# Block scores of the prompt computed per query in small matmuls, and the sample gates spread by a matmul, in a stage of a hybrid decoder step

## The chip, the cores and the metric

The kernel runs on one core of one Trainium2 chip. The metric is the device time of one execution in microseconds (us), the median of several runs. A core has a matrix engine (TensorE, PE in the profile; its weight loads are listed apart as PEld), a vector engine (VectorE, DVE), a scalar engine (ScalarE, ACT), GpSimd (POOL) and SyncE (SP), which here only issues DMA transfers. Each engine runs its own list of instructions in order and waits for the others on semaphores. SBUF is the on-chip memory with 128 partitions, PSUM the memory that TensorE writes.

## The reference, cut to what matters

One decoder layer for a prompt of 1024 tokens and for 8 samples of 4 new tokens with a history of 8192. Half of the heads do dilated window attention (mixer A), the other half native sparse attention (mixer B) with three branches that are weighted by gates. The change touches two things of mixer B.

For the prompt, the compressed branch: every query of 8 heads scores 16 compressed keys (one for each block of 64 tokens), adds a bias, masks blocks that have not ended, takes a softmax and multiplies the compressed values.

For the samples, the gates of all three branches:

```
gates = jax.nn.sigmoid(gates.astype(jnp.float32)).reshape(n, t, G_B, R_B, 3)

def _nsa_compressed(q, kc, vc, q_pos, bias_b):
    nbc = kc.shape[1]
    blk_end = (jnp.arange(nbc) + 1) * NSA_BLOCK - 1
    rel = q_pos[:, None] - blk_end[None, :]
    bias = jnp.transpose(bias_b[_t5_bucket(rel)], (0, 2, 3, 1))
    logits = jnp.einsum('ntgrd,nkgd->ntgrk', q, kc, ...) * ATT_SCALE + bias
    probs, _ = _masked_softmax(logits, (rel >= 0)[None, :, None, None, :])
    out = jnp.einsum('ntgrk,nkgd->ntgrd', probs, vc.astype(jnp.float32))
    return out, jnp.sum(probs, axis=3)
```

Here n is 1, t is 1024 for the prompt, g is 2 and r is 4 (8 query heads on 2 key heads), d is 64 and k is 16.

## The kernel before, in words

The program is a row of stages with a barrier of all engines between two of them: `front` (projections and compression), `compressed_and_dilated` (the stage of this change), `sample_selected`, `prompt_attention` and `ffn`. All numbers are 32-bit floats; TensorE does each such matmul in two passes, and the profile lists each pass as one MATMUL with one LDWEIGHTS. A transpose with the identity is one pass.

`compressed_and_dilated` interleaves three works in steps s = 0 to 11, an order that is written out by hand in a loop of each engine.

- The dilated attention of the 8 samples is the backbone. In step s, `keys(s, h)` transposes the keys of sample s in 8 banks of four 128 x 128 blocks (h = 0 and 1 are the halves) into two PSUM banks in turn (`psT`). ScalarE copies banks 0, 2, 4, 6 and VectorE banks 1, 3, 5, 7 to SBUF (`KT`, in the tile `turned`; `key_copies`). TensorE writes a bank again only when its last copy is done. `scores(n, h)` then multiplies. After the fourth sample VectorE takes a maximum over `psS`, ScalarE the exponential (`PR`), and `probs(g)` and `values(g)` follow.
- The compressed branch of the samples gives the choice of blocks (`choice`, its result is `pen`). SyncE waits for `pen` before it loads the rest of the values (items 12 to 15 of `load`), and from item 13 on also for `values(0)`. At the end SyncE issues the loads for the next stage (window keys, biases), and the stage ends when the last of its issues is done.
- The compressed branch of the prompt uses what is left. `qp` holds the queries with channels on partitions: chunk ch of four has two heads of 64 channels, 1024 tokens wide. `kbd` holds the 16 compressed keys twice, block diagonal, so that one matmul scores two heads and makes 32 rows. In step 3 `prompt_scores` makes the scores with `kbd` as weights (128 x 32) and the queries moving (512 columns); four chunks stand side by side in the array (`tile_position`). ScalarE and VectorE copy the two halves to `SQ`, which takes the place of chunk 0 of `qp`. In step 4 `prompt_scores_by_query` transposes the eight 128 x 128 blocks, so that queries are on partitions, and VectorE adds the bias of distance (`prompt_sums`), which makes `Lp`, 8 tiles of 128 queries with 8 heads and 16 blocks. `prompt_maxima` takes the maxima and subtracts them, ScalarE takes the exponential at the start of step 5, `prompt_weights` normalizes.

The sample gates: 768 numbers of one row in DRAM are sent by one DMA to all 128 partitions of `graw`. ScalarE takes the sigmoid in step 2, and `gates_and_block_logits` of VectorE sorts them with 24 small copies into `GB`. `graw` is a view of the tile `early`.

Of the kernel before, what the change touches and what calls it, by code (L numbers as in the profile page):

```python
# [9 lines left out]
ACT = mybir.ActivationFunctionType  # L10
AXX = mybir.AxisListType.X

P = 128
D = 1024
KC = D // P
SEQ = 1024
# [1190 lines left out]
def compressed_and_dilated(nc, io, scr, mixB, GB, Qb, pre, ident, kcs, vcs, knew, s_nl, s_mixed, stores):  # L1207
# [13 lines left out]
    with ExitStack() as stack:  # L1221
        m = Mem(nc, stack, "cd")
        flip = m.sb("flip", [P, P])
        rsum = m.sb("rsum", [P, 2, NR])
        qs = m.sb("qs", [P, 4, RS])
# [5 lines left out]
        graw = early[:, :].rearrange("p (a n) -> p a n", a=2)  # L1231
# [25 lines left out]
        SQ = qp[:, 0, :]  # L1257
# [31 lines left out]
        s_ps = m.sem("prompt_scores_by_block")  # L1289
        s_pa = m.sem("prompt_scores_copied_by_act")  # L1290
        s_pd = m.sem("prompt_scores_copied_by_dve")
# [69 lines left out]
        def _(pool):  # L1361
# [9 lines left out]
            pool.wait_ge(s_z, 4)  # L1371
# [13 lines left out]
        def _(sp):  # L1385
            def load(i):
                if i >= NS:
# [5 lines left out]
                         bass.AP(scr["gates"].tensor, SEQ * 24, [[0, P], [1, RS * 24]])).then_inc(s_c, 16)  # L1393
# [44 lines left out]
        def _(pe):  # L1438
# [78 lines left out]
            def gates_and_block_scores():  # L1517
                pe.wait_ge(s_c, LOADS)
                pe.wait_ge(s_z, 4)
# [13 lines left out]
            def prompt_scores():  # L1533
# [5 lines left out]
                for half in range(2):  # L1539
                    for ch in range(4):  # L1540
                        mm = pe.matmul(psX[32 * ch:32 * ch + 32, half, :], kbd[:, ch // 2, :],
                                       qp[:, ch, half * 512:half * 512 + 512], start=True, stop=True,
                                       tile_position=(0, 32 * ch))
                    mm.then_inc(s_ps, 1)

            def prompt_scores_by_query():
                pe.wait_ge(s_pa, 1)
                pe.wait_ge(s_pd, 1)
                for qt in range(QT):
                    pe.transpose(psX[:, qt // 4, (qt % 4) * P:(qt % 4) * P + P], SQ[:, qt * P:qt * P + P],  # L1550
                                 ident[:, :]).then_inc(s_po, 1)
# [50 lines left out]
            for s in range(NB + 4):  # L1602
# [9 lines left out]
                if s == 4:  # L1612
                    prompt_scores_by_query()
# [33 lines left out]
        def _(act):  # L1647
# [3 lines left out]
            for s in range(NB + 4):  # L1651
                if s < NB:
                    key_copies(act, copy, d_ca, 0, s, 0)
                if s == 5:
                    act.wait_ge(s_d, 3)
                    nc.scalar.activation(Lp[:, :, :, :], Lp[:, :, :, :], ACT.Exp).then_inc(s_e, 1)
# [24 lines left out]
                if s == 3:  # L1681
# [5 lines left out]
                    act.wait_ge(s_ps, 2)  # L1687
                    copy(SQ[:, 0:512], psX[:, 0, :]).then_inc(s_pa, 1)
# [13 lines left out]
        def _(dve):  # L1702
            def gates_and_block_logits():
                dve.wait_ge(s_a, 1)
# [87 lines left out]
            for s in range(NB + 4):  # L1792
# [25 lines left out]
                if s == 4:  # L1818
                    prompt_sums()
# [32 lines left out]
                if s == 4:  # L1852
                    prompt_maxima()
                    block_probs()
# [1539 lines left out]
```

## Time and profile before

| | |
|---|---|
| median of 3 runs | 2150.55 us (2150.45 to 2152.93) |
| the profiled execution's own time | 2152.93 us |
| its span, first to last instruction | 2151.2 us |
| PE busy | 2051.5 us (95%) |
| PEld busy | 1339.3 us (62%) |
| DVE busy | 1082.9 us (50%) |
| ACT busy | 521.6 us (24%) |
| POOL busy | 532.7 us (25%) |
| mean granted TensorE clock | 0.981 of full speed |

Times inside the execution are counted from the span's start. The stage of the change lies between 512.5 and 635.5 us. A row of the timeline gives the start, the length, the engine, the line, the operation, output <- input with their shapes, the number of instructions merged in it, and in brackets for how long the engine had been idle and who released it. "issue" names no releaser: the engine waited for nothing that the profile shows.

### The profile page before, as it was taken

What the parts mean: (1) busy time and instruction counts of PE and PEld (TensorE: products, weight loads), DVE (VectorE), ACT (ScalarE), POOL (GpSimd) and SP (SyncE); (2) the same over time, 40 slices, a digit from 0 to 9 for tenths busy, and PEclk for the clock granted to TensorE, in tenths of its full rate; (3) what the DMA queues carried; (4) which work ended last, traced back from release to release, by engine and by line L of the source; (5) the groups of instructions that cost most, each with busy time, mean ns of one, the idle gap of its engine ahead of it and who ended that gap; (6) DMA issues with size and microseconds to landing.
All of it is one profiled execution on the core that took longest, in us unless ns stands there. A gap on an engine that the chain in (4) does not pass through costs nothing. (4 is left out here: it accounts for less than half of the span.)

```text
span 2151.2 us, 31682 instructions
## 1 busy us (share of the span) xinstructions
PE 2051.5 (95%) x12366; PEld 1339.3 (62%) x12366; DVE 1082.9 (50%) x2484; ACT 521.6 (24%) x1106; POOL 532.7 (25%) x714
## 2 busy tenths in 40 slices
PE   6999999998977997999999999999999999999998
PEld 3445466665545665666676447888888888734443
DVE  5035455411525455666776226767777765611452
ACT  4111011001323344766766111011111111000011
POOL 1444234202024551012222101222322222303110
PEclk9999999998999998999999999999999999999999
DMA  8477678643697996222251414666556622601100
GB/s 219 138 241 258 243 294 305 236 170 109 231 339 290 402 396 226 99 67 68 82 155 39 133 60 156 215 208 204 196 196 211 220 79 60 227 12 30 42 40 39
DMA packets 156393, 373.05 MB, mean 173 GB/s; under 512 B 36981, under 2 KB 95085, under 8 KB 138189
## 3 DMA queue, kind: packets, MB, share of 16 engines
q1 hardware_dynamic: 126580, 149.89, 22.2%
q0 software_dynamic: 25280, 149.44, 18.0%
q10 hardware_dynamic: 4384, 71.68, 9.5%
q8 instruction: 99, 1.62, 0.3%
q14 instruction: 50, 0.41, 0.1%
HBM read 343.68 MB, written 98.60 MB: 206 GB/s over the span
## 5 line engine op out<-in xcount | busy, mean ns | idle before, releaser
L2773 PE MATMUL ff_ps<-ff_hx,whole_aw 128*128 128x264 f32 x2464 | 550.5, 386 | 0.9 <-DVE ff_hx L3074 0.9
L2773 PEld LDWEIGHTS ff_ps<-ff_hx,whole_aw 128*128 128x128 f32 x2464 | 467.1, 190 | 80.8 <-issue 1.4
L802 DVE STREAM_TRANSPOSE whole_space<-whole_space 128x512 f32<-128x512 f32 x256 | 155.3, 674 | 153.7 <-PE in_psH L611 142.0
L575 PE MATMUL in_ps<-in_w,in_xT 128*128 128x512 f32 (+1 forms) x512 | 201.5, 547 | 0.0
L1155 DVE CUSTOM_DVE_ANT_0 pa_L<-pa_psS,whole_space 128x512 f32<-128x512 f32 (+3 forms) x288 | 138.9, 532 | 46.8 <-PE pa_psS L1008 45.8
L575 PEld LDWEIGHTS in_ps<-in_w,in_xT 128*128 128x128 f32 x512 | 95.0, 190 | 94.2 <-issue 87.6
L1135 ACT ACTIVATE pa_L<-pa_L,pa_nm 128x640 f32<-128x640 f32 (+3 forms) x192 | 141.9, 741 | 32.3 <-DVE pa_nm L1165 30.5
L2799 PE MATMUL ff_ps<-ff_hx,whole_space 128*128 128x512 f32 x336 | 148.0, 593 | 0.0
L700 ACT ACTIVATE in_yout<-in_ps 128x128 f32<-128x128 f32 (+5 forms) x88 | 41.0, 479 | 378.8 <-PE in_ps L575 199.6
L3155 DVE SCALAR_TENSOR_TENSOR whole_space<-whole_space,ff_kept 128x1024 f32<-128x1024 f32 x88 | 123.3, 1401 | 3.1
L611 PE MATMUL in_psH<-whole_space 128*64 128x256 f32 (+1 forms) x1152 | 121.6, 364 | 0.0
L1008 PE MATMUL pa_psS<-whole_space,pa_qT 64*128 64x512 f32 (+3 forms) x576 | 115.3, 506 | 5.6 <-POOL pa_qT L1079 5.6
L589 PE MATMUL in_ps<-in_xT,in_w 128*128 128x352 f32 x384 | 117.6, 463 | 0.0
L2799 PEld LDWEIGHTS ff_ps<-ff_hx,whole_space 128*128 128x128 f32 x336 | 63.6, 190 | 80.6 <-issue 80.6
L2996 ACT ACTIVATE whole_space<-whole_space 128x1056 f32<-128x1056 f32 x22 | 23.8, 1084 | 368.6 <-DVE whole_space L3157 368.6
L1029 PE MATMUL pa_psT<-whole_ident,pa_L 128*128 128x128 f32 x816 | 111.9, 281 | 0.2 <-DVE pa_PT L1181 0.2
L1029 PEld LDWEIGHTS pa_psT<-whole_ident,pa_L 128*128 128x128 f32 x816 | 87.3, 141 | 39.5 <-issue 18.3
L2728 PE MATMUL ff_ps<-whole_space 128*128 128x512 f32 x256 | 111.2, 593 | 0.0
L1049 PE MATMUL pa_psO<-pa_PT,whole_space 128*64 128x128 f32 x1632 | 110.3, 279 | 0.9 <-DVE pa_tmp L1193 0.5
L1129 ACT ACTIVATE pa_PT<-pa_psT 128x512 f32<-128x512 f32 (+2 forms) x182 | 91.9, 541 | 75.9 <-PE pa_psT L1029 74.3
L611 PEld LDWEIGHTS in_psH<-whole_space 128*64 128x64 f32 x1152 | 74.9, 137 | 47.1 <-issue 13.0
L589 PEld LDWEIGHTS in_ps<-in_xT,in_w 128*128 128x128 f32 x384 | 71.8, 190 | 42.2 <-issue 3.8
(411 smaller groups left out, 2579.9 us busy)
## 6 DMA issues: line engine op xcount, KB each, us to landing
out_new_a_k_s<-in_cache_a_k ACTq DMA_DIRECT2D x8, 4088.0 KB
out_new_a_v_s<-in_cache_a_v ACTq DMA_DIRECT2D x8, 4088.0 KB
whole_aw<-in_w_up SPq DMA_DIRECT2D x44, 512.0 KB
in_w<-in_w_in SPq DMA_DIRECT2D x5, 2048.0 KB
whole_space<-in_cache_a_k SPq DMA_DIRECT2D x8, 1024.0 KB
whole_space<-in_cache_a_v SPq DMA_DIRECT2D x8, 1024.0 KB
ff_hx<-in_w_down SPq DMA_DIRECT2D x14, 512.0 KB, 4.7
whole_space<-in_x_prompt SPq DMA_DIRECT2D x13, 512.0 KB, 4.0
```

What stands on the lines that cost most here:

```text
L575: mm = pe.matmul(ps[0:n, b, 0:width], xT[:, k, t * P:t * P + n], w[:, at % WBUF, k, 0:width], start=(k == 0), stop=(k == KC - 1))
L589: mm = pe.matmul(ps[:, b, 0:n], w[:, at % WBUF, k, c * P:c * P + P], xT[:, k, r0:r0 + n], start=(k == 0), stop=(k == KC - 1))
L611: mm = pe.matmul(psH[dh * HD:dh * HD + HD, r % 2, o0:o0 + n], w1[:, kv, t16, dh, :], rows[:, dh, t, :], start=(t16 == 0), stop=(t16 == 15) ...
L802: last = dve.transpose(put[:, dh, :, k * HD:k * HD + HD].rearrange("p t (g b) -> p t g b", g=2), got[:, :, :, dh, :])
L1008: pe.matmul(psS[:, c % 2, h, 0:w], qT[r, i, qt * P:qt * P + P], kT[i][r, j0 * P + k0:j0 * P + k0 + w], start=True, stop=True).then_inc(s_q ...
L1029: mm = pe.transpose(psT[:, b % 3, (x - x0) * P:(x - x0) * P + P], turned, ident[:, :])
L1135: nc.scalar.activation(x, x, ACT.Exp, bias=nm[:, s, h:h + 1], scale=1.0, accum_out=sm[:, s, h:h + 1]).then_inc(s_ex, 1)
L1155: dve.tensor_tensor_reduce(L[:, u % 3, h, 512 * x:512 * x + n], psS[:, c % 2, h, 0:n], T[it % 2][:, h, SEQ - w + 512 * x:SEQ - w + 512 * x ...
L2728: mm = pe.matmul(ps[:, j % 6, :], mixT[:, k, t * P:t * P + P], wo[:, k, half * 512:half * 512 + 512], start=(k == 0), stop=(k == KC - 1))
L2773: mm = pe.matmul(ps[:, bank_of(x, j, g), 0:H2], aw[:, j % 2, at, k, :], hx[:, bt, k, g * H2:g * H2 + H2], start=(k == 0), stop=(k == KH - 1))
L2799: mm = pe.matmul(ps[:, b, :], a[:, k, :], wd(k0 + k)[:, c0:c0 + 512], start=(k == 0), stop=(k == KD - 1))
L3155: dve.scalar_tensor_tensor(out=out[:, 0:SEQ], in0=U[:, v, k:k + SEQ], scalar=tap(k), in1=out[:, 0:SEQ], op0=ALU.mult, op1=ALU.add)
```

## The change

Five edits, all in `compressed_and_dilated`:

1. `prompt_scores` takes the queries as weights (128 x 128) and `kbd` as the moving side (32 columns), for each of 8 query tiles and 4 chunks. The result has queries on partitions at once. `prompt_scores_by_query`, the tile `SQ` and the two copies into it go.
2. `prompt_sums` and `prompt_maxima` of VectorE, which stood at two places of step 4, stand behind the bias copy at the end of step 3, in `prompt_logits`.
3. The exponential of `Lp` on ScalarE stands at the end of step 4 and not at the start of step 5.
4. The gates come by DMA to one partition only; ScalarE takes the sigmoid there; TensorE spreads them over 128 partitions with two matmuls of a row of ones (1 x 128 weights, 384 columns); VectorE's 24 copies read them from PSUM.
5. GpSimd fills the row of ones, one memset more.

```
+        ones = m.sb("ones", [1, P])
-        graw = early[:, :].rearrange("p (a n) -> p a n", a=2)
+        graw = early[0:1, :].rearrange("p (a n) -> p a n", a=2)
...
+            pool.memset(ones[:, :], 1.0).then_inc(s_z, 1)
-            pool.wait_ge(s_z, 4)
+            pool.wait_ge(s_z, 5)
...
-                         bass.AP(scr["gates"].tensor, SEQ * 24, [[0, P], [1, RS * 24]])).then_inc(s_c, 16)
+                         bass.AP(scr["gates"].tensor, SEQ * 24, [[0, 1], [1, RS * 24]])).then_inc(s_c, 16)
...
             def gates_and_block_scores():
                 pe.wait_ge(s_c, LOADS)
-                pe.wait_ge(s_z, 4)
+                pe.wait_ge(s_z, 5)
+                pe.wait_ge(s_a, 1)
+                for a in range(2):
+                    pe.matmul(psX[:, a, 0:RS * 24 // 2], ones[:, :], graw[:, a, :], start=True, stop=True)
                 pe.transpose(psX[:, 0, 384:512], rows[:, :], ident[:, :]).then_inc(s_pe, 1)
...
                 pe.wait_ge(s_v, 7)
-                for half in range(2):
+                for qt in range(QT):
                     for ch in range(4):
-                        mm = pe.matmul(psX[32 * ch:32 * ch + 32, half, :], kbd[:, ch // 2, :],
-                                       qp[:, ch, half * 512:half * 512 + 512], start=True, stop=True,
-                                       tile_position=(0, 32 * ch))
-                    mm.then_inc(s_ps, 1)
-
-            def prompt_scores_by_query():
-                pe.wait_ge(s_pa, 1)
-                pe.wait_ge(s_pd, 1)
-                for qt in range(QT):
-                    pe.transpose(psX[:, qt // 4, (qt % 4) * P:(qt % 4) * P + P], SQ[:, qt * P:qt * P + P],
-                                 ident[:, :]).then_inc(s_po, 1)
+                        o = (qt % 4) * P + ch * 32
+                        mm = pe.matmul(psX[:, qt // 4, o:o + 32], qp[:, ch, qt * P:qt * P + P], kbd[:, ch // 2, :],
+                                       start=True, stop=True)
+                    mm.then_inc(s_po, 1)
...
-                if s == 5:
-                    act.wait_ge(s_d, 3)
-                    nc.scalar.activation(Lp[:, :, :, :], Lp[:, :, :, :], ACT.Exp).then_inc(s_e, 1)
...
-                    act.wait_ge(s_ps, 2)
-                    copy(SQ[:, 0:512], psX[:, 0, :]).then_inc(s_pa, 1)
+                if s == 4:
+                    act.wait_ge(s_d, 3)
+                    nc.scalar.activation(Lp[:, :, :, :], Lp[:, :, :, :], ACT.Exp).then_inc(s_e, 1)
...
             def gates_and_block_logits():
-                dve.wait_ge(s_a, 1)
+                dve.wait_ge(s_pe, 1)
                 for a in range(2):
-                    got = graw[:, a, :].rearrange("p (b t g n) -> p b g t n", b=4, t=NT, g=2)
+                    got = psX[:, a, 0:RS * 24 // 2].rearrange("p (b t g n) -> p b g t n", b=4, t=NT, g=2)
...
             def prompt_logits():
...
-                dve.wait_ge(s_ps, 2)
-                dve.tensor_copy(SQ[:, 512:1024], psX[:, 1, :]).then_inc(s_pd, 1)
-
-            def prompt_sums():
...
-            def prompt_maxima():
                 dve.wait_ge(s_L, QT)
```

How TensorE's instructions stand. The piece runs from the end of the keys of sample 3 to `scores(4, 0)`; cd_psT is the bank of key transposes, cd_psS holds the scores of the dilated attention, cd_psX the PSUM of the compressed branch, whole_space the loaded keys. Before:

```order
L1478 MATMUL cd_psS<-sample_turned,cd_QX 32x512 x4
L1535 MATMUL cd_psX<-cd_hank,cd_flip 128x128
L1541 MATMUL cd_psX<-cd_qp,cd_kbd 32x512 x8
L1459 MATMUL cd_psT<-whole_ident,whole_space 128x128 x16
L1478 MATMUL cd_psS<-sample_turned,cd_QX 32x388 x4
L1550 MATMUL cd_psX<-whole_ident,cd_qp 128x128 x8
L1459 MATMUL cd_psT<-whole_ident,whole_space 128x128 x12
```

Now:

```order
L1476 MATMUL cd_psS<-sample_turned,cd_QX 32x512 x4
L1536 MATMUL cd_psX<-cd_hank,cd_flip 128x128
L1543 MATMUL cd_psX<-cd_kbd,cd_qp 128x32 x32
L1457 MATMUL cd_psT<-whole_ident,whole_space 128x128 x16
L1476 MATMUL cd_psS<-sample_turned,cd_QX 32x388 x4
L1457 MATMUL cd_psT<-whole_ident,whole_space 128x128 x12
```

Eight matmuls and eight transposes have become 32 matmuls, all ahead of the keys of sample 4.

How VectorE's instructions stand at the same place, from the copy of the bias (cd_TB) to the first copies of sample 5; cd_Lp are the prompt's logits, sample_turned the copied keys. The rows of the eight sums that lie between the first and the last are left out here. Before, up to the second half of sample 4:

```order
L1722 COPY cd_TB<-cd_psX 128x128
L1724 COPY cd_qp<-cd_psX 128x512
L1644 COPY sample_turned<-cd_psT 128x4x128 x2
L1815 TENSOR_REDUCE cd_mx<-cd_psS 128x1
L1817 TENSOR_SCALAR cd_nm<-cd_mx 128x1
L1731 TENSOR_TENSOR cd_Lp<-cd_psX,cd_TB 128x8x2
```

and behind the eight sums:

```order
L1644 COPY sample_turned<-cd_psT 128x4x128
L1644 COPY sample_turned<-cd_psT 128x4x4
L1737 TENSOR_REDUCE cd_mxp<-cd_Lp 128x64
L1740 TENSOR_SCALAR cd_mcp<-cd_mxp 128x64
L1743 TENSOR_TENSOR cd_Lp<-cd_Lp,cd_mcp 128x1024
```

Now, from the last of the eight sums on:

```order
L1716 TENSOR_TENSOR cd_Lp<-cd_psX,cd_TB 128x128
L1720 TENSOR_REDUCE cd_mxp<-cd_Lp 128x64
L1723 TENSOR_SCALAR cd_mcp<-cd_mxp 128x64
L1726 TENSOR_TENSOR cd_Lp<-cd_Lp,cd_mcp 128x1024
L1636 COPY sample_turned<-cd_psT 128x4x128 x2
L1798 TENSOR_REDUCE cd_mx<-cd_psS 128x1
```

The sums, the maxima and the subtraction have moved ahead of the first key copies of sample 4.

## Rows read from the trace of the kernel before

**Rows 1.** Waits of TensorE on the key copies, 512 to 632 (us in total, times, longest)

```profile
PE cd_psT L1459 <- ACT sample_turned L1649: 3.6, 11, 1.1
PE cd_psT L1459 <- DVE sample_turned L1644: 2.1, 3, 1.7
```

**Rows 2.** Timeline, end of the stage, SyncE and VectorE, 616 to 637

```profile
616.16 10.59 SPq L1427 DMA_DIRECT2D whole_space<-in_cache_win_k  x2
626.39 0.46 DVE L1808 COPY cd_mixA<-cd_psT 64x64 f32<-64x64 f32 x2 [0.75 <-PE cd_psT L1514]
634.07 0.39 SPq L1434 DMA_DIRECT2D scr_mixT<-cd_mixA  x1
636.05 2.87 SPq L2005 DMA_DIRECT2D whole_space<-in_cache_win_v  x2
```

**Rows 3.** Waits of SyncE's queue, 512 to 632 (the same columns)

```profile
SPq L1414 <- DVE cd_pen L1779: 13.7, 1, 13.7
SPq L152 <- PE cd_psT L1459: 4.0, 4, 2.6
```

**Rows 4.** Timeline, step 2: TensorE, ScalarE and VectorE, 547 to 554.5

```profile
547.05 0.84 ACT L1679 ACTIVATE cd_early<-cd_early 128x768 f32<-128x768 f32 x1
547.64 0.33 PE L1520 MATMUL cd_psX<-whole_ident,cd_rows 128*128 128x128 f32 x1 [0.83 <-DVE sel_BS L1837]
548.78 2.49 DVE L1710 COPY sample_GB<-cd_early 128x32 f32<-128x32 f32 x24
549.02 0.46 PE L1524 MATMUL cd_psX<-whole_ident,cd_biasC 128*128 128x128 f32 x2 [1.06 <-DVE cd_biasC L1847]
550.58 1.57 PEld L1459 LDWEIGHTS cd_psT<-whole_ident,whole_space 128*128 128x128 f32 x8 [0.23 <-issue]
552.58 0.69 DVE L1644 COPY sample_turned<-cd_psT 128x512 f32<-128x512 f32 x1 [0.53 <-PE cd_psT L1459]
553.33 0.66 PEld L1459 LDWEIGHTS cd_psT<-whole_ident,whole_space 128*128 128x128 f32 x4 [0.23 <-DVE sample_turned L1644]
554.15 0.86 PE L1478 MATMUL cd_psS<-sample_turned,cd_QX 128*32 128x388 f32 x8
```

**Rows 5.** Timeline, steps 3 and 4: TensorE and VectorE, 559 to 567.4

```profile
559.14 0.19 PEld L1541 LDWEIGHTS cd_psX<-cd_qp,cd_kbd 128*32 128x32 f32 x8 [0.64 <-issue]
561.03 0.85 PEld L1459 LDWEIGHTS cd_psT<-whole_ident,whole_space 128*128 128x128 f32 x8 [0.84 <-issue]
563.49 0.86 PE L1478 MATMUL cd_psS<-sample_turned,cd_QX 128*32 128x388 f32 x8
565.62 1.21 DVE L1731 TENSOR_TENSOR cd_Lp<-cd_psX,cd_TB 128x16 f32<-128x16 f32 x8
567.38 0.99 PE L1459 MATMUL cd_psT<-whole_ident,whole_space 128*128 128x128 f32 x8 [1.13 <-ACT sample_turned L1649]
```

**Rows 6.** The same timeline, the maxima and what follows, 568 to 574

```profile
568.50 1.21 DVE L1737 TENSOR_REDUCE cd_mxp<-cd_Lp 128x64 f32<-128x1024 f32 x1
569.97 1.22 DVE L1743 TENSOR_TENSOR cd_Lp<-cd_Lp,cd_mcp 128x1024 f32<-128x1024 f32 x1
572.44 0.42 PEld L1459 LDWEIGHTS cd_psT<-whole_ident,whole_space 128*128 128x128 f32 x4 [0.42 <-DVE sample_turned L1644]
```

**Rows 7.** Weight loads of 128 x 128 with 32 moving columns, their followers, and small matmuls

```profile
594.48 1.86 PEld L1566 LDWEIGHTS cd_psX<-cd_early,sample_vcs 128*128 128x128 f32 x16 [0.84 <-issue]
596.18 0.94 PEld L1574 LDWEIGHTS cd_psX<-whole_ident,cd_Lp 128*128 128x128 f32 x8
...
1187.26 2.84 PE ff_ps L2824 x44
```

**Rows 8.** Stretches of 1 to 3 us: busy PE, PEld, DVE, ACT, POOL, granted clock, DMA share, GB/s

```profile
548.00:549.00 1.00, 0.00 (x0) 0.01 (x1) 0.97 (x12) 0.15 (x1) 0.00 (x0) 1.00 0.52 129
551.00:552.00 1.00, 1.00 (x7) 1.00 (x6) 0.96 (x7) 0.27 (x1) 0.00 (x0) 0.50 0.78 209
594.00:596.00 2.00, 2.00 (x22) 1.52 (x14) 0.00 (x0) 0.00 (x0) 0.00 (x0) 1.00 1.05 400
```

More of the change, by code:

```diff
@@ L1255, in compressed_and_dilated @@
         rgp = m.sb("rgp", [P, QT, HB])
-        SQ = qp[:, 0, :]
         PTp = qp[:, 0, :]
@@ L1288, in compressed_and_dilated @@
         s_a = m.sem("act")
-        s_ps = m.sem("prompt_scores_by_block")
-        s_pa = m.sem("prompt_scores_copied_by_act")
-        s_pd = m.sem("prompt_scores_copied_by_dve")
         s_po = m.sem("prompt_scores")
@@ L1611, in _ @@
                     scores(s - 1, 1)
-                if s == 4:
-                    prompt_scores_by_query()
                 if s < NB:
@@ L1711, in gates_and_block_logits @@
                     last.then_inc(s_v, 1)
-                dve.wait_ge(s_pe, 1)
                 dve.tensor_copy(hank[:, :, :], psX[:, 0, 384:512].rearrange("p (h e) -> p h e", h=HB)).then_inc(s_v, 1)
@@ L1817, in _ @@
                         dve.tensor_scalar(nm[:, g:g + 1], mx[:, g:g + 1], -1.0, None, ALU.mult).then_inc(d_nm, 1)
-                if s == 4:
-                    prompt_sums()
                 if s < NB:
@@ L1839, in _ @@
                     dve.wait_ge(s_c, LOADS)
-                    dve.wait_ge(s_z, 4)
+                    dve.wait_ge(s_z, 5)
                     for g in range(2):
@@ L1852, in _ @@
                 if s == 4:
-                    prompt_maxima()
                     block_probs()
```

## The prediction

> **What bounds the kernel now.** TensorE is busy for 95% of the span, but the question is what the stage from 512.5 to 635.5 waits for. I read the timeline of that stage first, then the waits, then the chain's end. In the stage TensorE has the longest list and nobody's result comes long before it is used: it waits only for the copies of transposed keys, 3.6 us in 11 times on ScalarE and 2.1 us in 3 times on VectorE [rows 1], and the other engines wait for it. So what is put into TensorE's list there, or between a bank and its copy, moves all that follows. What follows is tied to it: SyncE waits 13.7 us for the choice (`pen`, VectorE, behind TensorE's block sums) and another 4.0 us for keys and values of TensorE before it issues the loads of the second half [rows 3]. The stage's end is SyncE's: VectorE's last work starts at 626.39, SyncE issues until 634.46, 10.59 us of it in the two window loads [rows 2]. The two loads of the next stage's window values, of the same size, take 2.87 us to issue [rows 2], so about 7.7 us of the 10.59 look like a queue that is full of earlier loads. Those were released by the choice and by `values(0)`, hence by TensorE too. I therefore take a delay of TensorE in steps 2 to 5 to reach the end in full.
>
> **The gates (edit 4), +0.4.** TensorE idles from 547.97 (the transpose of `rows` at 547.64 is one instruction) to 549.02, where the bias is ready [rows 4]. The two new matmuls wait for the sigmoid, which ends at 547.89 [rows 4]. Two matmuls are four passes of 384 columns. The prompt's old scores give the price of columns: 16 passes of 512, four side by side, from 559.14 to 561.03, so 0.47 us each at most [rows 5]; for 384 columns that is 0.35, four make 1.4. TensorE is through them at about 549.3 and through the transpose at 549.45: 0.4 late. VectorE's 24 copies, which used to start at 548.78, now wait for that transpose, plus its flight of 0.33 [rows 4]: start at about 549.65, 0.9 later. A copy costs 2.49/24 = 0.104 us from SBUF [rows 4]. No row has these copies from PSUM; the nearest is the eight sums, which read 16 to 128 elements of PSUM, 72 in the mean, in 1.21/8 = 0.151 us [rows 5]. The 40 elements more than 32 account for about 0.04 of it, at the 1.22 us for 1024 elements of the subtraction [rows 6]. That leaves 0.10 to 0.11: I take no extra. Bounds: nothing, and 24 x (0.151 - 0.104) = 1.1 us. VectorE is then 0.9 late for the key copy of 552.58, on which TensorE waited until 553.33; it had been idle for 0.53 before that copy [rows 4], so 0.4 to 0.5 arrives at TensorE. The term is 0.4, from 0 to 1.6.
>
> The Trainium skill speaks against this edit: "VectorE: DVE Perf Modes", section on the TRN2 errata, gives VectorE a fixed part of 58 cycles from SBUF and 120 from PSUM at 0.96 GHz, so 65 ns more a copy. By that rule (an estimate of mine from its table) the 24 copies would cost 1.5 us more and the sum would be 1.5 higher. The row of the eight sums does not bear it out for copies that stand in a row: I go by the row.
>
> The clock: the stretch with an idle TensorE (548 to 549: busy 0.00) was followed by a granted clock of 0.50 at 551 to 552, the 1.2 GHz level [rows 8]. The new matmuls fill a part of that gap. If the clock stays, the gain is at most what it cost: from 550.58 to the scores at 554.15 it took 3.57 us [rows 4], for the same instructions at full clock 561.03 to 563.49, 2.46 us [rows 5]: 1.1. But VectorE's copy is late anyhow, so I count 0 and keep -0.7.
>
> **The scores (edit 1) on TensorE, +4.9.** Before, 559.14 to 561.03: 1.89 us [rows 5]. Now 32 matmuls are 64 passes, each with its own weight load of 128 x 128. The same shape stands in the trace at L1566: 16 such loads, the next group's first load starts at 596.18, the first of these at 594.48, so 1.70/16 = 0.106 us each [rows 7]. 64 x 0.106 = 6.8 us, 4.9 more. Bounds: the 20 x 20 matmuls, 44 in 2.84 us or 0.065 each [rows 7], 4.1 us and so +2.3; the loads at half clock, 8 in 1.57 or 0.196 each [rows 4], 12.6 us and +10.7.
>
> **The eight transposes that go (step 4), 0.** Eight transposes take 0.99 us (those at 567.38), but that bank waited for ScalarE's exponential and copy in any case, with 1.13 us of idle time [rows 5]: the idle time grows by what they leave. ScalarE waits for VectorE's maximum over `psS`, which does not depend on them. The two copies into `SQ` that go stood ahead of key copies whose bank was not ready earlier: 0 too.
>
> **The moved sums and maxima (edit 2), +2.6.** This is the wait that the change adds. Queued behind the subtraction on VectorE are the key copies of sample 4, banks 1 and 3; TensorE's bank 3 waits for the copy of bank 1. Counted from the start of the scores, S: TensorE is through at S + 6.8, the last result lands at S + 7.05. The first four sums run under the second half of the matmuls; the last four, the long ones, 416 of the 576 elements, take 0.75 of the 1.21 us [rows 5], to S + 7.85. Then maximum, negation limit and subtraction, from 568.50 to 571.19 = 2.69 us [rows 6]: S + 10.6. The copy of bank 1, 0.69 [rows 4]: S + 11.3. Bank 3's four transposes, 0.42 and about 0.2 around them [rows 6]: the scores start at S + 11.9. Before, they started at 563.49 - 559.14 = S + 4.35 [rows 5]. Difference 7.5, of which 4.9 is the matmuls and 2.6 this. Upper bound: all 1.21 + 2.69 behind the matmuls, +0.5 more; lower bound: nothing of it, if the copies stood ready otherwise, 0.
>
> **What the places left free give, -0.3.** In step 5 TensorE waited until 572.44 for a VectorE copy that stood behind the subtraction, which ended at 571.19, and the probabilities; the idle time before it is 0.42 [rows 6], against 0.23 at the same bank of sample 3 [rows 4]. With the subtraction gone from there 0.2 to 0.4 comes back, I take 0.3. The exponential (edit 3) now runs while TensorE does `scores(4, 0)` and the next bank and ScalarE has no bank to copy: 0. Without that cover it would cost its length, about that of VectorE's pass over the same 1024 elements, 1.22 [rows 6]. The memset (edit 5) and the smaller DMA are done tens of us before they are needed: 0.
>
> **The new gap, +0.7.** Bank 3 would start 1.9 us after the keys' start (2.46 from there to the scores [rows 5], less 0.6 for the bank), at S + 8.7; it starts at S + 11.3. TensorE is idle for these 2.6 us while VectorE works off its list. A shorter idle time was followed by half clock at 551 [rows 8], at a cost of up to 1.1 as above. It may or may not come again; the row nearest to it says it does, and a part of the slowed work is hidden by ScalarE's copies. I take 0.7, from 0 to 1.1.
>
> **Sum.** 0.4 + 4.9 + 2.6 - 0.3 + 0.7 = 8.3 us. On the profiled execution's own 2152.93 us (span 2151.2) that makes 2161.2. That execution was the slowest of the three; on the median of 2150.55 it is 2158.9, which is my forecast: 0.39% slower. A difference of less than 0.2%, 4.3 us, can hardly be told from none for this kernel.
>
> **Rivals.**
>
> *Half clock through the scores.* In 64 passes of 32 columns the array moves little, and the clock may fall. The 2 us of the same shape ran at 1.00 [rows 8], but they were short; the new stretch is more than three times as long. Price: 12.6 instead of 6.8 us [rows 4], so 14.1 in all, 2164.7. The Trainium skill says in "TensorE: Matmul & The Clock Gate", part 1, that throttled is the default and activity lifts it; whether weight loads with few columns are activity enough no run here shows.
>
> *Cheap passes.* If loads hide better in a long row, 0.065 us as in the small matmuls: 4.1 us instead of 6.8, in all 5.6, 2156.2. Against it: those load 20 rows, and L1566 with the same shape as here is at 0.106.
>
> *The stage's end absorbs it (not slower).* SyncE's window loads cost 7.7 us more to issue than later ones of the same size. If that is because old transfers fill the queue, and these are through before SyncE comes (because TensorE is later and they are not), the 10.59 shrink towards 2.87 and the end moves by 8.3 - 7.7 = 0.6: 2151.2, or 2149.9 with the clock kept at the gates as well. It decides if the backlog has drained by the first window load. Against it: the transfers in the queue are released by the choice and by `values(0)`, which move by the same 8 us.
>
> **Chances.** The forecast 0.70, its own range 2156.5 to 2161.5 (the pass price 0.106 up to 1.97/16, the clock's 0 to 1.1, the copies' 0 to 1.1); half clock 0.12; cheap passes 0.08; absorbed 0.10. The range for 8 in 10 leaves out the absorbed end and most of what lies above the half clock: 2154.5 to 2165. Slower by over 0.2% (above 2154.9): forecast, half clock, cheap passes less a little, 0.88. Within 0.2%: most of the absorbed case and the rest, 0.10. Faster (below 2146.2): 0.02.
>
> **What the new profile would show.** Right: 64 loads over 6.5 to 7.5 us at L1543; a wait of TensorE of 2 to 3 us on VectorE's key copy after them, released by a copy behind the subtraction L1726; the gap before the bank that waits for ScalarE longer by the transposes' 0.8; the last issue of SyncE at about 642.5. Wrong: a granted clock of 0.50 under L1543 (then the half clock); a pitch far from 0.106; a window load issue far below 10.59 us with the end near 635 (absorbed); or a gates step that costs over 1.6 us, which would give the page on VectorE its due.

## The result, and the profile after

The changed kernel takes 2166.11 us (median of 6 runs, 2163.24 to 2169.78), the kernel before 2150.5 in the runs beside it: a difference of 15.6 us. The ratio on record is 1.0081, 95% interval 1.0068 to 1.0094; it is an estimate for which 35 runs of the changed kernel are listed, and not the quotient of these two medians (1.0073). The ratios below are such estimates too. The changed kernel is 0.7 to 0.8% slower. Forecast were 2158.9 us and a range up to 2165.0: the direction was right, the size about half of what came, and the time lies above the range. The profiled execution of the changed kernel took 2163.33 us, its span is 2161.5 us.

The page of the changed kernel, busy times and the queue that carries instructions (packets, MB, share of 16 engines):

```profile
PE 2060.7 (95%) x12410; PEld 1349.1 (62%) x12410; DVE 1079.5 (50%) x2483; ACT 520.6 (24%) x1105; POOL 538.1 (25%) x715
...
q8 instruction: 99, 1.62, 0.3%
```

TensorE has 44 passes more than before (12,410 against 12,366), and as many loads: 64 for the scores and 4 for the gates come, 16 and 8 go. In what follows 2.65 us are taken off times of the stage after, since everything up to the last copy into `BS` in step 2 ran that much later in this execution (549.54 against 546.89), with no edit of TensorE's, ScalarE's or VectorE's lists ahead of it; the stage itself began 2.5 us later.

The gates, timeline of TensorE and VectorE after [rows 4]:

```profile
550.69 1.52 PE L1520 MATMUL cd_psX<-cd_early,cd_ones 1*128 1x384 f32 x4 [1.24 <-ACT cd_early L1668]
552.51 2.44 DVE L1700 COPY sample_GB<-cd_psX 128x32 f32<-128x32 f32 x24 [0.99 <-PE cd_psX L1521]
557.43 0.86 PE L1476 MATMUL cd_psS<-sample_turned,cd_QX 128*32 128x388 f32 x8
```

The scores that stood at 554.15 are at 557.43, so 0.63 late when the 2.65 are taken off. The scores of the prompt, the keys behind them and the wait that the moved list makes, TensorE and its loads after [rows 5, 6]:

```profile
562.42 9.68 PEld L1543 LDWEIGHTS cd_psX<-cd_kbd,cd_qp 128*128 128x128 f32 x64 [0.64 <-issue]
571.84 1.76 PEld L1457 LDWEIGHTS cd_psT<-whole_ident,whole_space 128*128 128x128 f32 x8
576.46 1.12 PE L1457 MATMUL cd_psT<-whole_ident,whole_space 128*128 128x128 f32 x4 [1.51 <-DVE sample_turned L1636]
577.51 1.52 PE L1476 MATMUL cd_psS<-sample_turned,cd_QX 128*32 128x388 f32 x8
582.05 1.00 PE L1457 MATMUL cd_psT<-whole_ident,whole_space 128*128 128x128 f32 x8 [1.25 <-ACT sample_turned L1641]
593.91 0.80 PEld L1488 LDWEIGHTS cd_psT<-whole_ident,cd_PR 128*128 128x128 f32 x8 [0.84 <-issue]
```

From the first score load to the keys' first load it takes 9.42 us, against 1.89. The granted clock says why. Windows after (time, then busy PE, PEld, DVE, ACT, POOL with counts, clock, DMA share, GB/s) [rows 8]:

```profile
564.00:566.00 2.00, 2.00 (x20) 2.00 (x20) 0.00 (x0) 0.00 (x0) 0.00 (x0) 1.00 1.05 391
566.00:568.00 2.00, 2.00 (x16) 2.00 (x15) 0.52 (x4) 0.00 (x0) 0.00 (x0) 0.72 1.05 379
568.00:570.00 2.00, 2.00 (x11) 2.00 (x11) 0.00 (x0) 0.00 (x0) 0.00 (x0) 0.50 1.09 396
...
577.00:580.00 3.00, 3.00 (x16) 1.42 (x15) 1.60 (x2) 0.00 (x0) 0.00 (x0) 0.50 0.03 11
```

At full clock 20 passes go in 2 us, 0.100 each. TensorE is busy without a break, and yet the grant falls to 0.50 (the 1.2 GHz level), where 11 passes go in 2 us, 0.18 each. It falls at 566.9, 4.5 us after the first load, and is back at 580.5, so the keys and the first scores of sample 4 run under it; from 584.0 to 587.4 it is down once more.

VectorE's list behind the passes, after [rows 5, 6]:

```profile
566.28 0.52 DVE L1716 TENSOR_TENSOR cd_Lp<-cd_psX,cd_TB 128x16 f32<-128x16 f32 x4 [3.98 <-PE cd_psX L1543]
572.27 0.78 DVE L1716 TENSOR_TENSOR cd_Lp<-cd_psX,cd_TB 128x80 f32<-128x80 f32 x4 [5.47 <-PE cd_psX L1543]
573.09 1.22 DVE L1720 TENSOR_REDUCE cd_mxp<-cd_Lp 128x64 f32<-128x1024 f32 x1
574.58 1.22 DVE L1726 TENSOR_TENSOR cd_Lp<-cd_Lp,cd_mcp 128x1024 f32<-128x1024 f32 x1
575.72 0.68 DVE L1636 COPY sample_turned<-cd_psT 128x512 f32<-128x512 f32 x1
```

And the stage's end, SyncE after [rows 2], with the wait for the choice, which was 13.7 us [rows 3]:

```profile
632.89 11.45 SPq L1425 DMA_DIRECT2D whole_space<-in_cache_win_k  x2
650.76 0.39 SPq L1432 DMA_DIRECT2D scr_mixT<-cd_mixA  x1
```

```profile
SPq L1412 <- DVE cd_pen L1762: 15.2, 1, 15.2
```

The last issue moved from 634.07 to 650.76, 16.7 us, so 14.0 in the stage (14.2 if one counts from the stage's first matmul, as the experiments below do). By places (each counted with the 2.65 taken off): gates 0.6; the 64 passes 7.5; from the keys of sample 4 to their scores at 577.50 (563.49 before) 3.2, from there to the transposes of `PR` at 593.91 (577.92 before) 2.0; the rest of the stage 0.7.

One more place shows, 130 us later and in a stage that no edit touches. TensorE's row of values in the selected attention, in the changed kernel:

```profile
777.69 3.45 PE L2158 MATMUL sb_psV<-whole_space,sb_PT 128*32 128x128 f32 x118
782.26 0.62 PE L2158 MATMUL sb_psV<-whole_space,sb_PT 128*32 128x128 f32 x10 [1.12 <-issue]
...
799.76 3.66 PE L2158 MATMUL sb_psV<-whole_space,sb_PT 128*32 128x128 f32 x125
804.69 0.41 PE L2158 MATMUL sb_psV<-whole_space,sb_PT 128*32 128x128 f32 x3 [1.26 <-issue]
```

The same row in the kernel before runs through:

```profile
768.51 3.68 PE L2178 MATMUL sb_psV<-whole_space,sb_PT 128*32 128x128 f32 x128
```

TensorE stops in the middle of 128 equal passes, with no semaphore behind it. From 640 to 840 the waits put down to "issue" are 2.7 us after and 0.2 before. The spans of the two profiled executions differ by 10.3 us only, less than the medians: in before's, the first large exponential of this stage came 40.4 us after SyncE's last issue of the stage ahead, in after's 36.0. That is not the change's doing: a second profile of the changed kernel (below) has 42.7. What differs is a wait of TensorE for the transfer of window values, 2.7 us in before's profile, none in after's and 3.0 in the second; more of it behind the experiments.

### The profile page after: what moved, and what is told of

Its sections match the earlier page's. It is cut to its first block and busy times, and to the rows that moved or that the text cites. A ratio compares the mean times of both kernels' runs of the same rounds, so it can differ in the third digit from the quotient of the medians.

```text
span 2161.5 us, 31769 instructions
## 1 busy us (share of the span) xinstructions
PE 2060.7 (95%) x12410; PEld 1349.1 (62%) x12410; DVE 1079.5 (50%) x2483; ACT 520.6 (24%) x1105; POOL 538.1 (25%) x715
## 3 DMA queue, kind: packets, MB, share of 16 engines
q8 instruction: 99, 1.62, 0.3%
## 5 line engine op out<-in xcount | busy, mean ns | idle before, releaser
L700 ACT ACTIVATE in_yout<-in_ps 128x128 f32<-128x128 f32 (+5 forms) x88 | 40.9, 479 | 378.8 <-PE in_ps L575 199.5
```

## The experiments

Each median stands against runs of the kernel before that were measured together with it. "In the stage" is the time from the stage's first matmul to SyncE's last issue in the one profiled execution; it is 121.5 us for before and 135.7 after. Two kernels below that leave the stage's work as it was have 123.4 and 122.9, so a single such figure is good to about 2 us.

**The scores only.** The change with the old gates (edits 4 and 5 undone):

```
-                pe.wait_ge(s_a, 1)
-                for a in range(2):
-                    pe.matmul(psX[:, a, 0:RS * 24 // 2], ones[:, :], graw[:, a, :], start=True, stop=True)
```

> The change without the gates part (edits 4 and 5): scores with 32 moving columns, sums and maxima at the end of step 3. Clock theory: the 64 passes of 32 columns leave the array so little used that the granted clock falls to 0.50 about 5 us into them and stays there through the wait on VectorE; this happens here as well. In the change's trace the gates part accounts for 0.6 us (554.15 became 557.43, less the 2.65 by which the stage began later), so the median is some 15 us above before, 2165.5, and TensorE's passes take 9 to 10 us. Rival, gates: the gates matmuls cost several us by where they put the clock's fall; then 2160 or less. Rival, forecast as it stood: 0.106 us per pass, 6.8 us, total +8, 2158.

Measured: 2169.75 us, ratio 1.0103 (1.0087 to 1.0119), 134.8 us in the stage. The passes took 9.26 us, as expected; the median is 4 us above the expected 2165.5. Nothing is saved by undoing the gates; the loss is in the scores and what moved with them.

**The gates only.** The kernel before with edits 4 and 5.

> The kernel before with the gates part alone (edits 4 and 5). Clock theory: the gates part is worth only its 0.6 us, 2151.1; VectorE's 24 copies from PSUM take 2.4 to 2.5 us as in the change's trace. Rival, gates: several us more than that, 2154 or more. The page's rule of a longer fixed part from PSUM would give copies of 4.0 us in all and about 2152.5.

Measured: 2150.49 us, ratio 1.0009 (0.9994 to 1.0024). In its trace the stage takes 123.9 us, and the transposes of `PR` come 0.7 us later in the stage than before; the clock falls in step 2 as it did. This is the term as forecast.

**The scores alone, list left late.** Edit 1 with the sums, maxima and the exponential where they stood (the piece shows VectorE's list against the scores only):

```
                 if s == 4:
+                    prompt_sums()
...
+                    prompt_maxima()
                     block_probs()
```

> The kernel before with edit 1 alone: scores with 32 moving columns, but VectorE's sums, maxima and subtraction and ScalarE's exponential stay where they were in steps 4 and 5. Clock theory: the clock falls in the passes all the same (9 to 10 us instead of 1.9, +7.5), and the transposes and scores of step 4 run at half clock (+1.5 to +3); no wait on VectorE's list behind the passes: +9 to +11, 2160.5. Rival, moved list: the wait behind the passes is what matters and the clock falls because of it, not in the passes; then the passes take 6.8 us at full clock and the total is +5, 2155.5.

Measured: 2163.53 us, ratio 1.0066 (1.0047 to 1.0085), 131.4 us in the stage, 3.4 less than with the moved list. So two thirds of the loss or more belong to the passes; their loads took 9.16 us here. That is as the clock theory has it, but the whole, 14.1 us, is more than the expected 9 to 11; the stage's part of it, 10.0, is not.

**A wide moving side.** The scores only, but `kbd` is [128, 4, 128] with zeros outside each chunk's 32 columns, so that each pass moves 128 columns and the four chunks are summed in PSUM. Passes and loads of TensorE are as many as before, and GpSimd issues four small loads of keys more:

```
-                        mm = pe.matmul(psX[:, qt // 4, o:o + 32], qp[:, ch, qt * P:qt * P + P], kbd[:, ch // 2, :],
-                                       start=True, stop=True)
+                        mm = pe.matmul(psX[:, qt // 4, o:o + P], qp[:, ch, qt * P:qt * P + P], kbd[:, ch, :],
+                                       start=(ch == 0), stop=(ch == 3))
```

> As the change without its gates part, but the moving side is 128 columns wide and not 32: the keys stand block diagonal for each chunk with zeros in the other 96 columns, and the four chunks accumulate. The same 64 weight loads, four times the moving columns, the same result. Clock theory: with four times the columns the clock stays at 1.00 through the passes, they take 6.8 to 7.6 us, and the total is 2 to 6 us below the version with 32 columns, 2156 to 2163. Rival, passes alone: columns only cost; the passes take as long as or longer than with 32 columns (over 9 us), the total is the same or higher, 2165.5 or more.

The same stretch, first in the scores-only kernel (passes from 558.32), then here (from 558.17):

```profile
562.00:564.00 2.00, 2.00 (x17) 2.00 (x16) 0.52 (x4) 0.00 (x0) 0.00 (x0) 0.81 1.05 385
564.00:566.00 2.00, 2.00 (x11) 2.00 (x11) 0.00 (x0) 0.00 (x0) 0.00 (x0) 0.50 1.06 389
```

```profile
562.00:564.00 2.00, 2.00 (x20) 2.00 (x20) 0.52 (x4) 0.00 (x0) 0.00 (x0) 1.00 1.05 386
564.00:566.00 2.00, 2.00 (x20) 2.00 (x20) 0.41 (x3) 0.00 (x0) 0.00 (x0) 1.00 1.09 395
...
570.00:572.00 2.00, 2.00 (x12) 0.50 (x10) 0.69 (x1) 0.00 (x0) 0.00 (x0) 0.50 1.05 386
```

The passes and bank 3 of the keys there, in the timeline:

```profile
558.14 7.22 PEld L1540 LDWEIGHTS cd_psX<-cd_kbd,cd_qp 128*128 128x128 f32 x64 [0.64 <-issue]
...
569.77 0.93 PE L1457 MATMUL cd_psT<-whole_ident,whole_space 128*128 128x128 f32 x4 [2.44 <-DVE sample_turned L1633]
```

With four times the columns per load the clock holds through all 64 passes, and they take 7.22 us instead of 9.26. The loads are the same in number and size, so the fall under them hangs on what the passes move. But the grant falls now at 570.0, right behind TensorE's wait for VectorE's list, which grew from 1.61 to 2.44 us and ended at 569.8, and the stage is only 1.4 us shorter (133.4). The median, 2168.51 us (ratio 1.0099, 1.0083 to 1.0114), can't be told from the scores only: the clock and the passes came as the clock theory has them, but the expected 2156 to 2163 did not.

**Wide moving side, list left late.** The third kernel with the fourth's `kbd`.

> Scores with 128 moving columns (zeros in 96 of them) and VectorE's and ScalarE's steps left where they were before (no edit 2, 3, 4, 5). Clock theory, in its form after the first four runs (the clock falls either in passes of 32 columns or in the wait on VectorE's moved list): neither is here, the clock stays at 1.00 through steps 3 and 4, the passes take 7.2 us, +5.3 in the stage, 2155. Rival, passes: the 64 weight loads themselves bring the late half-clock spells whatever the columns; then 2160 or more, as with edit 1 alone (2163.5).

Measured: 2164.98 us, ratio 1.0069 (1.0055 to 1.0083). Loads 7.22 us, 129.3 us in the stage, 2.2 less than with 32 columns. The clock held until 574.0, behind the passes, the keys and the scores of sample 4; the expected 2155 was missed by 10 us all the same, and in the median nothing of the faster passes shows.

**The list early, scores as before.** Edits 2 and 3 without 1: the eight transposes, sums and maxima in step 3, the exponential at the end of step 4.

```
                     prompt_scores()
+                    prompt_scores_by_query()
...
                     prompt_logits()
+                    prompt_sums()
+                    prompt_maxima()
```

> The old scores (eight matmuls side by side, copies to SQ, eight transposes), but the transposes at once in step 3, and VectorE's sums, maxima and subtraction and ScalarE's exponential where the change has them. It is edits 2 and 3 without edit 1. Theory that the moved list is a cost of its own: TensorE waits for the copies (0.85 us), does the transposes (1.0) and then idles about 2.9 us in front of bank 3; +4.8 in the stage at full clock, and the clock falls in that idle time, +1 to +2: 2155.5 to 2156.5. Rival, that the list costs only together with the slow passes: at most +2, 2151.5.

Measured: 2157.66 us, ratio 1.0049 (1.0035 to 1.0063), 127.9 us in the stage (+6.4, expected 4.8 and 1 to 2 for the clock), no stop in a values row of the selected attention. TensorE waits 2.50 us for VectorE, and the clock falls near the end of that wait (564.2). An order of the list that adds no instruction costs half as much as the change.

**The passes in two halves.** Old gates; 32 passes in step 3, 32 in step 4 at the place of the transposes, the sums and maxima at the end of step 4.

> 32-column passes as in the change, but in two halves of 32 passes: query tiles 0 to 3 in step 3, tiles 4 to 7 in step 4 where the transposes stood; VectorE's sums and maxima at the end of step 4, the exponential in step 5; old gates. Clock theory: neither half is long enough to bring the clock down (in the change it fell 5 us into the passes), each half takes 3.4 us, 1.5 more in step 3 and about 1.4 more in step 4 after the idle time there is used up: +3, 2152.5. Rival, clock falls in any such stretch: each half 4.5 us or more and +7 or more, 2157.

Measured: 2166.4 us, ratio 1.0077 (1.0064 to 1.0091). Each half took 3.65 us, that is full clock, and the stage was 131.3 us. Shorter stretches keep the clock too, but the median is no better than with all the passes in a row, 14 us above the expected 2152.5.

**The change again**, beside the last three:

> The whole change again beside these three, since the version without its gates part came out at 2169.8 and the change at 2166.1. Both theories: 2166 to 2169; the trace again shows the clock at 0.50 before the passes end. If the gates part helps when it comes with the scores, this stays below 2167 with the passes at 9.4 us or less.

Measured: 2166.62 us, ratio 1.0082 (1.0068 to 1.0095), 134.3 us in the stage. The clock fell earlier this time, 3.6 us after the first load, and the passes took 10.56 us:

```profile
558.27 10.56 PE L1543 MATMUL cd_psX<-cd_kbd,cd_qp 128*128 128x32 f32 x64 [0.48 <-DVE cd_TB L1711]
```

By now the medians of all kernels with 64 passes lay 1.4 to 7.7 us further above before than their stages do. All of them have the stops in the values rows, and the places follow a rule. In the row of 128 passes they lie after 118 and 125 passes in both profiles of the change (44 passes added), after 115 and 122 in the kernels with 40 added, always 250 passes apart, whenever the stage began. The next four kernels test whether the number of instructions ahead is the cause.

**Before, with 44 more passes.**

```
+            wait_copied(use["out", 1])
+            for _ in range(22):
+                pe.matmul(psT[0:32, use["out", 1] % 2, 0:1], ident[:, 0:32], ident[:, 0:1], start=True, stop=True)
```

> The kernel before with 22 small matmuls (two passes each, so 44 passes and 44 weight loads, one moving column, into a bank that nothing reads any more) at the end of TensorE's list of the stage, where it stands idle for 9.4 us in the trace of before (626.4 to 635.7). Nothing of the stage's work is moved. Theory A (instruction supply): in the change's two traces sample_selected's values rows stop after 118 and 125 of 128 passes for 1.1 and 1.3 us with no semaphore behind it, 250 passes apart; in the kernels with 40 added passes the stops stand after 115 and 122. So the place follows the count of instructions ahead of it. This kernel has the change's count: stops of over 1 us after 118 and 125 passes, and a median 2 to 4 us above before (2151.5 to 2153.5). Theory B (the stops come from the later start of the stage, by when its transfers collide): the stage ends when it did, no stop over 0.3 us there, median within 1 us of before.

```profile
766.20 3.45 PE L2181 MATMUL sb_psV<-whole_space,sb_PT 128*32 128x128 f32 x118
770.77 0.62 PE L2181 MATMUL sb_psV<-whole_space,sb_PT 128*32 128x128 f32 x10 [1.12 <-issue]
788.26 3.66 PE L2181 MATMUL sb_psV<-whole_space,sb_PT 128*32 128x128 f32 x125
793.21 0.41 PE L2181 MATMUL sb_psV<-whole_space,sb_PT 128*32 128x128 f32 x3 [1.28 <-issue]
```

The stops are those of the change, to the pass and within 0.02 us (1.12 and 1.28 against 1.12 and 1.26), in a kernel whose work is that of before. Median 2153.65 us against 2150.05, ratio 1.0016 (1.0006 to 1.0027): +3.6 us, 1.3 to 5.8. The DMA view of this kernel from 768.0 to 768.7, just ahead of the first stop (769.65 to 770.77), has a packet of the instruction queue, and so has 790.5 to 791.2 ahead of the second:

```profile
q8 instruction: 1, 0.02, 9.0%
```

**Before, with 250 more passes** (125 such matmuls), the control:

> The control: before with 125 such matmuls (250 passes). Theory A: no stop in a values row, median 2149 to 2151, as before. If the padding by itself costs (it keeps TensorE busy ahead of the next stage, or the stage's end waits for it), this kernel shows that cost, and e9 and e10 are read against it. Theory B: as before too.

Whole again, no stop in a row:

```profile
770.80 3.68 PE L2181 MATMUL sb_psV<-whole_space,sb_PT 128*32 128x128 f32 x128
```

The page has two instruction packets more than before for 250 passes and 250 loads:

```profile
q8 instruction: 101, 1.65, 0.3%
```

The median is 2155.68 us (1.0014 to 1.0045), against an expected 2149 to 2151, and the trace shows why: the padding doesn't fit. It runs until 641.2, and the next stage's first matmul starts 7.3 us after SyncE's last issue, against 1.65 in before. So 5.6 us is the price of a padding of this length. (The granted clock was 0.50 while it ran.)

**The change, with 206 more passes**, 250 more than before in all:

> The change with 103 such matmuls (206 passes) at the same idle place, so that 250 more passes stand ahead of sample_selected than in before: one whole distance between two stops. Theory A: the stops fall where before has them, that is nowhere in a values row; idle of TensorE put down to issue in sample_selected falls from 2.7 to under 1 us, and the median to 2162 to 2164.5. Theory B: the stops stay, 2166 to 2167. If the 206 passes and loads do not fit into the idle time, the next stage starts later by what is over; the trace shows it.

The stops are gone, as in the control:

```profile
772.88 3.68 PE L2161 MATMUL sb_psV<-whole_space,sb_PT 128*32 128x128 f32 x128
```

But the median is 2173.01 us (1.0066 to 1.0114, 6 runs from 2161.64 to 2176.35), above what either theory had. The padding's price is 5.2 us by this kernel's own trace (6.93 us from SyncE's last issue to the next stage's first matmul, against 1.78 in the change); less that it is 2167.9, and the 2 to 4 us that were expected back can't be seen. The place of the stops is settled by this run, their price is not: its profiled execution, the longest of the six, has a wait of 6.0 us for window values that the control doesn't have.

**Wide moving side, list late, with 206 more passes:**

> The kernel with the scores alone, wide moving side and late list (2164.98, 7.8 us longer in the stage by the profiled execution but 15.5 by the median), with 206 such passes at the same place. It had 40 passes more than before, so it stands at 246, 4 short of a whole distance. Its trace had 4.5 us of issue stops in sample_selected. Theory A: these fall under 1.5 us, median 2160 to 2162. Theory B: stays at 2164 to 2166.

No stop in a values row of the selected attention either; 2166.81 us (1.0042 to 1.0087). The padding costs 4.8 us by this trace; less that it is 2162.0, at the upper end of the expected 2160 to 2162 and 3.0 below the same kernel without padding, though the intervals overlap.

**Where TensorE stops, counted over the whole kernel.** If one counts the MATMUL records from the kernel's first, every stop of over 0.5 us that is put down to "issue" lies, in all 14 profiles, after 240 or 241 passes of a count by 250, or after 112 or 113 of it. The kernel before has one as well, after 3,363 passes, in the stage of the change; the changed kernel has none there and one after 3,491, and then those after 4,990 and 5,240 that were shown:

```profile
620.95 3.87 PE L1504 MATMUL cd_psO<-whole_space,cd_PT 128*32 128x128 f32 x116 [1.27 <-issue]
```

```profile
639.30 1.21 PE L1502 MATMUL cd_psO<-whole_space,cd_PT 128*32 128x128 f32 x32 [1.17 <-issue]
```

Not each of these places stops TensorE. In the kernel with 44 more passes the packet of 768.33 starts when 4,952 passes are done, and the 38 up to the stop take 1.3 us. In the kernel before, the packet at this place starts after 4,955, at 771.9, but slower instructions follow, TensorE comes to 4,990 only 4.4 us later, and there is no stop. In the changed kernel the place after 4,740 lies in the middle of a values row without a stop; its packet started at 758.75, 92 passes ahead. The kernels with 40 passes added have three such stops in `sample_selected` (after 4,740, 4,990 and 5,241), 3.0 to 3.9 us in all, where the change and the kernel with 44 have two, 2.4 us.

**What differs between executions.** From the first matmul of `sample_selected` to the first of `prompt_attention` it is 193.9 to 200.0 us in the eight profiles in which TensorE doesn't wait there for window values, and 199.5 to 206.3 in the six in which it does, for 2.0 to 6.0 us. Before (200.3) is one of the six, the change (194.4) is not; the change again (203.0) and the change with 206 more passes (203.3) are. Their waits, in this order:

```profile
PE sb_psV L2128 <- DMA whole_space<-in_cache_win_v: 2.7, 1, 2.7
```

```profile
PE sb_psV L2108 <- DMA whole_space<-in_cache_win_v: 3.0, 1, 3.0
```

```profile
PE sb_psV L2111 <- DMA whole_space<-in_cache_win_v: 6.0, 1, 6.0
```

The stages behind are within 2 us of each other in all profiles. So one profile says what happens in a stage, but its whole time is one draw: the profiled executions of the scores only and of the two halves are 7.5 and 9.6 us below their own medians. Of the nine profiles of kernels with the 64 passes five have this wait, of the five without them one. Whether the passes make it more frequent is not shown.

## Why the prediction was wrong

**The frame held.** The direction, slower, was right, and by the path that was given. TensorE's delay in steps 2 to 5 reached the end in full: 13.3 us at the transposes of `PR`, 14.0 at SyncE's last issue. The window loads took 11.45 us, not fewer than 10.59, so "absorbed" fell.

**Gates, +0.4: right.** 0.6 in the trace, and alone within its measurement of nothing. The 24 copies took 2.44 us from PSUM, 2.49 from SBUF [rows 4]. The Trainium skill's fixed part for PSUM ("VectorE: DVE Perf Modes", section on the TRN2 errata), which would have made 1.5 us, is not borne out for this row of copies. The clock's gain there was 0, as taken: the grant was at 0.50 from 550.4 to 553.9 before, and from 553.2 to 556.7 after.

**Scores, +4.9: the step that failed.** The pitch at full clock was right (0.100 measured, 0.106 taken); what failed is "the 2 us of the same shape ran at 1.00", taken as a reason for 1.00 over 7 us. The grant fell within the passes in both profiles of the change, 4.5 and 3.6 us after the first load, and the term became 7.5 and 8.3. The rival had the right mechanism at a chance of 0.12. Of the Trainium skill's "TensorE: Matmul & The Clock Gate", part 1 (throttled is the default, activity lifts it), the wide moving side is the nearest run: with the same loads in the same place the grant fell under 32 moving columns and not under 128. The page's rule agrees with that as far as it goes, and it spoke for the rival.

**The moved list and the new gap, +2.6 + 0.7 - 0.3: too small.** Measured 3.2 to the scores of sample 4 and 2.0 more to the transposes of `PR`. The mechanism was as told: keys' bank 3 waits for VectorE's copy, and this copy stands right behind the subtraction. The length of the wait was right too where the clock held: 2.6 us were forecast, and with 128 moving columns it was 2.44. But in the change the clock was already down and stayed there until 580.5, and it fell again from 584.0 to 587.4, so the keys and both scores behind ran at half. The next bank waited 1.25 us for ScalarE, 1.13 before, and not 0.8 longer, as was forecast for the transposes that go; in the scores only, where the clock had come back by then, it was 2.01, as forecast. With the list left late the stage is 3.4 us shorter; the list moved without the new passes costs 6.4 in the stage (this includes the transposes' move). The prediction had counted the half clock as one event of at most 1.1 us; that is the size that was wrong here.

**A term that was missing.** No step of the prediction looked at what 44 more passes and loads do to the stages behind. They shift two of the places where TensorE stops into rows that would otherwise run through. By the kernel that adds only that, it is 3.6 us (1.3 to 5.8), 2.4 of them visible as stops.

**The sum.** 14.0 and 3.6 make 17.6; the change's first median is 15.6 above before, and the ratio on record stands for 17.4. For the second measurement of the change it is 12.8 and 3.6, 16.4 against 17.1. Within the 2 us to which a stage figure is good, and the 1.3 to 5.8 of the other term, that closes. For the scores only, both wide kernels and the two halves, the stage plus 3.6 stays 3.4 to 4.1 us short of the median's distance. 0.6 to 1.5 of it are their third stop. The rest may be the wait for window values, or falls of the clock between 640 and 840, which differ between the two profiles of the change too; with one trace for each kernel that stays open. So does why the wide moving side shortens the stage and not the median: its 2.2 us with the list late stand against a wait of 4.3 us for window values in its profiled execution, and 2.0 in that with 32 columns.

## What to carry to other kernels

A long row of weight loads with few moving columns kept TensorE busy without a break here, and the clock still fell to the level that this kernel otherwise has behind idle times: price such a stretch at both levels, and the work behind it too. What is pulled forward on VectorE costs what stands behind it, in this kernel as much by itself as half of the change. And count instructions: when a change adds some, look for stops with "issue" in the middle of equal passes in later stages; padding that moves nothing else tells them from contention. And before two profiles are subtracted, look for a wait that one has and the other has not; here a wait for one transfer came and went between executions of the same kernel.

## What the runs showed of the hardware

- 64 loads of 128 x 128 with 32 moving columns: 9.2 to 10.5 us in a row with the clock falling to 0.50, 3.65 per 32 in two halves, 7.22 with 128 columns.
- TensorE's instructions come in packets: 1.62 MB in 99 for some 24,800 passes and loads, 16.4 KB each, so about 250 of them in one; 500 more make 101. Stops of TensorE of 0.6 to 2.8 us that are put down to "issue" lie, in all 14 profiles, only after 240 or 241, or 112 or 113, of each 250 passes, and by far not at each such place: where a packet started 38 passes ahead in a fast row (1.3 us) there was a stop, where the passes ahead took 4.4 us or were 92 there was none. The DMA share was 0.9 to 1.0 at the stops of the change. That the arrival is what TensorE waits for is inferred from the count and the packet's time; that the place goes with the count is shown.
- TensorE's wait for the transfer of window values early in `sample_selected` was 2.0 to 6.0 us in six profiled executions and absent in eight, and came and went between two executions of the changed kernel.
- 206 passes of one column and their loads of 128 x 32 took 11.15 us at a granted clock of 0.50, 0.054 each.
